# Dense attention's query blocks of the second and fourth pair of heads, in the order from wide to narrow

## The reference, cut to what matters

```python
def mla_attention(q_nope, q_rope, k_nope, k_rope, v):
    # 8 heads; queries and keys 64 + 32 = 96 wide, values 64 wide; L = 1024
    def one_block(bi):                     # 128 queries at a time, 8 blocks
        start = bi * Q_BLOCK
        logits = (jnp.einsum('bqhd,bshd->bhqs', qn, k_nope)
                  + jnp.einsum('bqhr,bsr->bhqs', qr, k_rope)).astype(jnp.float32) * B_QK_DIM ** -0.5
        causal = key_idx[None, :] <= q_idx[:, None]
        logits = jnp.where(causal[None, None], logits, NEG_INF)
        p = jax.nn.softmax(logits, axis=-1).astype(v.dtype)
        return jnp.einsum('bhqs,bshd->bqhd', p, v)
    out = lax.map(one_block, jnp.arange(L // Q_BLOCK))
    return jnp.moveaxis(out, 0, 1).reshape(bsz, L, B_WIDTH)
```

## Time and profile before

| | us |
|---|---|
| median of three runs | 2899.28 |
| lowest, highest run | 2897.71, 2907.05 |
| profiled execution, its own time | 2898.13 |
| span of the profiled execution | 2896.1 |
| TensorE busy in the span | 2805.3 (97%) |
| VectorE busy | 1472.4 (51%) |
| GpSimd busy | 1031.9 (36%) |
| ScalarE busy | 742.9 (26%) |

### The profile page before, as it was taken

The page is one execution under the profiler, slowest core; times in us unless marked ns, Lnnn a source line. Parts: engine busy times, 40 slices in busy tenths (PEclk is TensorE's granted clock), DMA queues, the critical chain, the costliest instruction groups (busy, mean ns, idle before and its releaser), DMA issues.

```text
span 2896.1 us, 36058 instructions
## 1 busy us (share of the span) xinstructions
PE 2805.3 (97%) x14772; PEld 2249.0 (78%) x14772; DVE 1472.4 (51%) x1829; ACT 742.9 (26%) x1094; POOL 1031.9 (36%) x451
## 2 busy tenths in 40 slices
PE   7999999999999999999999999899999999999998
PEld 4888888778888887776888466577887888888887
DVE  4853234652333334556999544996555423333324
ACT  5001124432111013454121456663111100011101
POOL 1433323454444444442132014001344434444434
PEclk9999999999999999999999999999999999999999
DMA  8531114223111123253132100002411111111112
GB/s 309 187 111 37 37 37 138 88 88 94 49 46 51 44 65 95 88 155 74 44 106 95 37 1 2 2 2 95 148 56 44 44 51 51 43 51 51 43 58 102
DMA packets 256235, 211.33 MB, mean 73 GB/s; under 512 B 23131, under 2 KB 240746, under 8 KB 255722
## 3 DMA queue, kind: packets, MB, share of 16 engines
q1 hardware_dynamic: 253082, 201.12, 22.6%
q10 hardware_dynamic: 3024, 8.39, 0.8%
HBM read 187.46 MB, written 20.97 MB: 72 GB/s over the span
## 4 chain that ended last, share of the span: by engine, by line
PE 79%; DVE 14%; ACT 3%; issue 2%; POOL 0%; DMA 0%; SPq 0%; ACTq 0%; DVEq 0%; POOLq 0%
PE PS L1161 18%; PE PS L1171 17%; PE PS L911 13%; PE PS L1107 9%; DVE MB L2439 6%; PE PS L1123 5%; PE PS L1408 3%; PE PS L895 3%; PE PS L1315 2%; PE PS L1373 2%; PE PS L1450 1%; DVE STEP L2543 1%; PE PS L1346 1%; DVE NMX L2577 1%; PE PS L1226 1%
## 5 line engine op out<-in xcount | busy, mean ns | idle before, releaser
L780 POOL TENSOR_TENSOR WHI<-RAW,ZERO 128x1024 fp32r<-128x1024 f32 x148 | 283.1, 1913 | 1160.6 <-PE PS L1161 284.9
L793 POOL TENSOR_TENSOR WLO<-RAW,WHI 128x1024 fp32r<-128x1024 f32 x112 | 270.1, 2412 | 476.6 <-ACT WHI L1566 476.6
L782 POOL TENSOR_TENSOR WLO<-RAW,WHI 128x1024 fp32r<-128x1024 f32 x148 | 406.8, 2749 | 11.6
L1680 ACT ACTIVATE RL<-PS 128x1024 f32<-128x1024 f32 x48 | 49.3, 1027 | 870.8 <-PE PS L1161 870.8
L911 PE MATMUL PS<-H,WHI 128*128 128x512 f32 x864 | 269.8, 394 | 2.4 <-DVE L L2592 0.9
L911 PE MATMUL PS<-L,WHI 128*128 128x512 f32 x864 | 267.3, 391 | 0.0
L911 PE MATMUL PS<-H,WLO 128*128 128x512 f32 x864 | 266.8, 390 | 0.0
L2354 DVE TENSOR_TENSOR FT<-RL 128x1024 f32<-128x1024 f32 x48 | 92.8, 1934 | 316.9 <-ACT RL L1680 316.9
L1566 ACT ACTIVATE WHI<-RAW 128x1024 fp32r<-128x1024 f32 x112 | 118.8, 1061 | 465.0 <-PE PS L1107 195.4
L1107 PE MATMUL PS<-H,WHI 128*128 128x512 f32 x512 | 202.1, 395 | 3.4 <-POOL WLO L793 1.9
L1107 PE MATMUL PS<-H,WLO 128*128 128x512 f32 x512 | 199.4, 390 | 0.0
(11 more groups left out here) (375 smaller groups left out, 5487.1 us busy)
## 6 DMA issues: line engine op xcount, KB each, us to landing
RAW<-w_fc SPq DMA_DIRECT2D x96, 512.0 KB, 3.9
RAW<-w_ff SPq DMA_DIRECT2D x68, 512.0 KB, 3.6
RAW<-w_in SPq DMA_DIRECT2D x62, 512.0 KB, 3.9
ADA<-w_ada SPq DMA_DIRECT2D x32, 512.0 KB, 5.0
RAW<-w_out SPq DMA_DIRECT2D x24, 512.0 KB, 4.0
ADA_FIRST<-w_ada SPq DMA_DIRECT2D x16, 512.0 KB, 9.7
X<-x_scratch SPq DMA_DIRECT2D x2, 4096.0 KB, 12.2
GB<-gate_scratch SPq DMA_DIRECT2D x8, 1024.0 KB, 6.1
```

What stands on the lines that cost most here:

```text
L780: nc.gpsimd.tensor_add(WHI[j][:, 0:n], RAW[j][:, 0:n], ZERO[:, 0:1].to_broadcast([P, n])).then_inc(s_whi, 1)
L782: nc.gpsimd.tensor_sub(WLO[j][:, 0:n], RAW[j][:, 0:n], WHI[j][:, 0:n].bitcast(F32)).then_inc(s_w, 1)
L793: nc.gpsimd.tensor_sub(WLO[w % 2][:, :], RAW[w % 2][:, :], WHI[w % 2][:, :].bitcast(F32)).then_inc(s_w, 1)
```

## The change

`ATT` takes its blocks for the second and fourth pair of heads from a second list, `(6, 7, 4, 5, 2, 3, 0, 1)`. Blocks still come in twos (6 and 7, 4 and 5, ...), since two of them share a bank and one multiplication into `YB`; the column at which that multiplication writes is taken from the same list. Each tile does what it did; only the numbers of the tiles change.

```diff
@@ -559,7 +559,8 @@
-        ATT = [(b, 2 * c + e) for c in range(4) for b in range(NB) for e in range(2)]
+        BLOCK_ORDER = [(0, 1, 2, 3, 4, 5, 6, 7), (6, 7, 4, 5, 2, 3, 0, 1)]
+        ATT = [(b, 2 * c + e) for c in range(4) for b in BLOCK_ORDER[c % 2] for e in range(2)]
         ATT += [(b, r + 4 * e) for b in range(NB) for r in range(4) for e in range(2)]
         PAIRS, PAIR_GROUPS, KEYS_AT, QK_SETUP = 64, 32, 52, 8
@@ -2520,7 +2521,7 @@
                 if g < 16:
-                    at = 2 * P * (g % 4)
+                    at = P * BLOCK_ORDER[g // 4 % 2][2 * (g % 4)]
                     V.tensor_mul(chunk(YB, g // 4)[:, at:at + 2 * P], src, inverse[:, :]).then_inc(s_oe, 1)
```

## The result

The changed kernel is slower by 0.21%: its ratio to the kernel before is 1.0021 with a 95% interval of 1.0014 to 1.0028 (+4.1 to +8.1 us). The medians are 2906.14 us of 20 runs and 2900.52 us of 20 runs of the kernel before beside them, 5.6 us apart. Predicted were 2903 us, in 2898 to 2909, as +4.0 us over a median of 2899.28. By the bound of 0.3% it is no change, as forecast, and its sign is the predicted one. The loss comes out larger than the sum of +4.0, which lies just under the interval; the traces show which step of the sum fell short. Two runs of the kernel before, beside those of e1 to e4, took 6447.65 and 16029.59 us, and the ratios are formed without them.

What follows compares the result with a forecast made beforehand. TensorE was busy 97% of the span, with GpSimd's chain to the sparse tiles hidden by only 0.34 us. GpSimd's end +3.8 and 0.2 for tile 65's matrices made +4.0 over 2899.28, about 2903 us, range 2898 to 2909.

Steps and rivals of the forecast that it cites:

- KHH comes later: Fourth pair: with wide blocks first, ScalarE starts KHH 16.6 us behind tile 48's logits instead of 10.0, 6.6 us late.
- GpSimd's chain is moved whole: From KHH to the sparse tiles: GpSimd's chain still lasts 31 us and ends 6.6 us later, at 1807.4.
- TensorE arrives at about 1802.5: First sparse tile, 64: TensorE gets there at 1802.5 instead of 1801.13, from +3.4, -4.8, +1.5 and +1.3.
- A wait of 5 us: Ahead of the first sparse logits: TensorE waits for GpSimd from about 1802.5 to 1807.5, where nothing was.
- The second pair is even: Tiles 16 to 48: waits of 2.3 us go, 2.0 come; net -0.3, bounds -1.5 to +2, taken as 0.
- The steps down cost 0.1 to 0.5: Inside a descending pair: stepping 7 to 4 costs 0.1, 5 to 2 0.3, 3 to 0 0.5; 1.3 with late exponentials.
- What comes back: Behind the wait: less work is left, so GpSimd's last QS write ends near 1818.8 against 1814.98, net +3.8; return 2 to 3.5.
- Rival B: Pause and narrow tiles: the half clock lasts longer behind GpSimd's end, total +7 to +9 us, 2907; chance 0.16.
- A: Rival, faster: GpSimd's chain isn't exposed and only waits at joins vanish, -4.5 to -6 us, about 2894; chance 0.10.
- C: Rival, absorbed: sparse tiles start ahead as TensorE has 3.4 us less left over; 0 to +1.5 us, about 2900; chance 0.18.

Runs made afterwards that it cites:

- e1: Changed kernel with only the fourth pair of heads going from wide to narrow, the second as before; 1.0033 of the kernel before.
- e4: Kernel before, old block order, with KEYS_AT 55 instead of 52, so ScalarE makes KHH later; 1.0020 of the kernel before.
- e3: Changed kernel with KEYS_AT 48 instead of 52, so ScalarE makes KHH earlier; 1.0004 of the kernel before.
- e2: Changed kernel with only the second pair of heads going from wide to narrow, the fourth as before; 1.0013 of the kernel before.
- e7: Changed kernel with six spare multiplications keeping TensorE busy ahead of the wait for GpSimd at tile 64; 1.0012 of the kernel before.
- e6: Changed kernel with the step matrices of tile 65 made in round 52 instead of round 64; 1.0021 of the kernel before.
- e5: Kernel before, old block order, with KEYS_AT 48 instead of 52, so ScalarE makes KHH earlier; 1.0002 of the kernel before.
- e11: Kernel before with the last quarter of QS filled with zeros by four short additions; one run, 2896.27 us.
- e10: Kernel before with 12 spare multiplications in TensorE's wait ahead of tile 68; 1.0005 of the kernel before.

## Why the prediction was right, and where its sum was short

*KHH comes later*: predicted 6.6 us, measured 6.88 (16.87 against 9.99). *GpSimd's chain is moved whole*: 31.26 us, right; e4 shows the same loss from lateness alone, e3 that the loss goes with it. *TensorE arrives at about 1802.5*, which is 42.95 behind tile 48's logits: its wait began 43.19 behind them. *A wait of 5 us*: 5.08. *The second pair is even*: from tile 16's logits to tile 48's -0.37 us (predicted -0.3); the +0.4 of e2 is a fall of the clock, and beside e4, which has it too, e2 is at -0.3. *The steps down cost 0.1 to 0.5*: 0.29, 0.43, 0.50, and 1.32 for the predicted 1.5 behind KHH. Up to the first sparse logits the sum is right: +6.3 from the first dense logits (predicted 1807.5 - 1801.13 = +6.4). It is +6.7 in the fourth pair and -0.4 in the second, which the sum had taken as 0.

*What comes back* is the step that failed. I had GpSimd's last write end 3.8 us late and let the tiles follow it, with 2.5 us regained and 0.2 lost to the matrices of tile 65. Measured, GpSimd's end was 4.76 us late, and tile 77 6.66: 1.6 of the 2.5 came back at GpSimd's end and was gone again at tile 77. Two things were mis-sized. The attend step and transposes behind the wait run at half clock, which put GpSimd's second clearing 2.63 us behind the first and not 1.6; with the clock held (e7) it is 1.68. And the state at GpSimd's end is not the same: it starts its last quarter sooner behind the first sparse logits (3.6 us, not 5.1), so VectorE comes to the matrices of tile 67 beside the whole of it and ends the 8.6 us with one tile fewer. They last 5.04 us, against 2.94 before. I had put this at 0.2 and on the wrong tile: e6 shows that tile 65's cost nothing. With the clock held 2.0 us come back, with GpSimd's work halved 2.3 us. In the two traces compared the clock comes back at about the same place (23.7 and 24.1 us behind the first sparse logits). Against the 30.6 and 31.0 of e2 and e5, where it comes back later, 0.8 to 1.3 of the 2.5 did come back, so the size of the miss is known to about 1 us only.

Rival B, the dearer clock, is thus right in that the pause's half clock costs, about 2 us, but wrong in its price of +7 to +9, and in part in the way. Its condition (half clock longer than 10 us behind GpSimd's end) was met only just: 0.87 in 1830 to 1840 puts the rise near 1832.6, 12 us behind GpSimd's end at 1820.8, before 10. And it charged TensorE's rate behind GpSimd's end, while e7's gain is there by tile 68, ahead of GpSimd's end. A needed a chain that isn't exposed; there was none: e4 and the wait of 5.08 speak against it. C, more absorbed, is contradicted: tile 77 is 6.66 us late, not 0 to 1.5. The forecast of 2903 held by its range. What the prediction had wrong here is its sentence that the half clock ahead of GpSimd's end is hidden behind GpSimd and mostly free: it cost the 2.0 us of e7.

What stays open: the 0.13% of e2, why the clock comes back at 23.7 us in one trace of the old order and at 26.5 or 27.4 in others with the same code there, and whether a start 0.3 us earlier of tile 67's matrices would by itself bring the 2 us.

## What to carry to other kernels

Reordering equal work still moves everything that is keyed to a position in it. Look for the preparations that another engine starts at a numbered step, measure their length against what is left of the stage, and move the step along with the order: here a slack of 0.34 us stood on a chain of 31 us. Less work behind a pause doesn't mean time regained, when the pause costs TensorE its clock and the stretch behind it hangs on two engines that get in each other's way. And before a stretch of two traces is compared, look where the clock came back in each: one stretch with the same code took 29.4, 30.6 and 31.0 us, enough to hide what e11 had gained by tile 71. When a wait is filled with spare work, check that the work ends before the wait does (e10).

## What the runs showed of the hardware

VectorE's step matrices, 0.7 to 0.9 us for four when GpSimd rests, took 5.88, 5.04 and 4.04 us beside GpSimd's additions, while maxima of 1024 columns from PSUM took 1.2 us with and without them, and the chain from KHH to GpSimd's last long write took 31.2 to 31.3 us in every run. The same four matrices of tile 67 took 2.9 to 3.0 us where they started 0.46 us ahead of GpSimd's additions, and 5.0 us where they started 0.19 or 0.08 us ahead. Keeping TensorE busy through a 5 us wait kept its clock at 1.00 there and brought 2.0 us in the 13 tiles behind it.
